# Linear attention beside a dense projection: the eighth group of scores behind the second unit of the tile in place of the first

## The chip, the cores and the metric

The kernel runs on one core of one Trainium2 chip. The metric is the device time of one execution in microseconds (us). Before the change it is 2720.19 us, the median of 3 runs (2718.54 to 2729.52).

## The reference, cut to what matters

Two transformer blocks over a sequence of 1024 tokens with width 1024, beside a context of 256 tokens. The first block is a gated linear attention in both directions with 4 heads (keys of 128, values of 256), together with a pooling branch; the second is a neighbourhood attention with a convolutional feed-forward part. The change touches the linear attention of the first block:

```python
p = h @ w_in                      # q, k, v, two low-rank gates, and the wide inputs zA, uB, zB, gA, gB
q, k = rope_2d(q), rope_2d(k)     # rotation by row and column
la = log_sigmoid(lowrank @ w_up + b) / 16        # decay per token and channel, forward and backward
...
diff = b[:, :, :, None, :] - b[:, :, None, :, :]  # b: cumulated decay
scores = einsum('bhid,bhjd,bhijd->bhij', q, k, exp(diff))   # within a chunk
S = exp(bC) * S + einsum('bhjd,bhjv->bhdv', k * exp(bC - b), v)   # state between chunks
```

## The kernel before

All work is written out engine by engine, each with its own queue in program order; semaphores join them. The dense products dominate. A weight tile (1024 x 128) is loaded by SP into `w_raw`, split by POOL into a high and a low part (`w_hi` L840, `w_lo` L843), and multiplied by TensorE as hi x hi + lo x hi + hi x lo. `pe_tile` (L484) does one tile: for each *unit* of 512 tokens `pe_unit` (L468, the matmuls at L478) issues 24 matmuls into one of two PSUM banks `pb`, and ScalarE evicts it (`store_tile`, L973). A unit waits for its bank (`bank_free`) and a tile for its split (`w_split`). The tile's first matmul raises `w_begun`, which lets POOL split the next tile. `pe_tile` takes a function `between`, which is called once, behind the first unit.

The first phase of the linear attention runs beside the dense tiles from number `T_ZA` on. It goes over ten chunks of 128 tokens: two of the context, without scores, and then eight of the sequence (`more`). Each chunk has three dense tiles of two units. In a chunk of the sequence, all 4 heads together:

- `p_gates` (L2691): the products for the decays (L2704) into banks 0 and 1 of `g`, and eight transposes of the values (L2712) into banks 2 and 3. The first wait for the fifth, the second for the seventh masked copy (`f_pred`) of the chunk before.
- VectorE then builds by levels, from small blocks to large, the keys and queries scaled by the decays (`f_first`, `f_grow`, L1880 to L1909), with ScalarE copying halves (`f_kept`); then two scans (`run`, L1959), two products for the state's keys (`kd`, L1964), and the masked copies.
- The scores within the chunk are made in eight *groups* (`p_scores`, L2715). Group 0 is the diagonal part, group m the level m - 1; each is one 128 x 128 product per head, into bank (m + 2) mod 6 of `g`. ScalarE copies group 0 into `pt` (L1152), and VectorE lays the groups 1 to 7 over it by seven masked copies (`f_choose`, L1932), each of which waits for its group (`f_lev`) and for the copy before it.
- Group 7 writes bank 3, which held group 1; so it waits for the first masked copy (L2736, `f_pred` at 7c + 1).
- `p_keys` (L2744): eight transposes of `kd` into banks 4 and 5 (L2753), which wait for `kd` and for the third masked copy.
- ScalarE stores `pt` behind the seventh copy, and then takes the transposed keys (`p_last`, L1096 to L1109).
- VectorE's queue goes on from the seventh copy to the rotation of the next chunk (`rope`, L1868 to L1871) and to the decays (L1945, L1880).

On TensorE, one chunk is: gates and value transposes, tile 0, tile 1, groups 0 to 3, first unit of tile 2, groups 4 to 7, second unit of tile 2, keys. After the last chunk TensorE goes on with the next dense tile; the other engines meet at the phase's end (`end_phase`), which ScalarE reaches when its stores have landed.

Of the kernel before, what the change touches and what calls it, by code (L numbers as in the profile page):

```python
# [95 lines left out]
def build(nc, modt, modw, cond, crow, cols, mats, tabs, hmask, inv, sgb, xT, ctxT, ctx2T, wall, wup, sgw, bias,  # L96
# [7 lines left out]
    with ctx:  # L104
# [296 lines left out]
        sq2, a = at("sq2", [P, 2, T], a)  # L401
        root2, a = at("root2", [P, T], a)
        _, a = at("xw", [P, KT, T], a)
        hh, a = at("hh", [P, 2, 2, T], a, F32R)
        hl, a = at("hl", [P, 2, 2, T], a, F32R)
# [56 lines left out]
        def step(base, i, by):  # L462

            return base if i is None else i * by + base
# [3 lines left out]
        def pe_unit(pe, b, xhi, xlo, tokens, kts, wcols, bank, ready=None):  # L468

            n = tokens.stop - tokens.start  # L470
            total, count = 3 * len(kts), 0
            first = None
            for k, wc in zip(kts, wcols):
                if ready is not None:
                    pe.wait_ge(xh_ready, ready + k)
                    pe.wait_ge(xl_ready, ready + k)
                for w, x in ((w_hi, xhi), (w_lo, xhi), (w_hi, xlo)):
                    mm = pe.matmul(pb[bank][:, 0:n], w[:, b, wc:wc + P], x[:, k, tokens],  # L478
                                   start=(count == 0), stop=(count == total - 1))
                    first = first or mm  # L480
                    count += 1
            return first, mm

        def pe_tile(pe, t0, i=None, tiles=0, units=0, xhi=None, xlo=None, ready=(), between=None, begin=0):  # L484

            b, u0 = t0 % 2, UNIT[t0]
            xhi, xlo = xhi or xh, xlo or xl
            pe.wait_ge(w_split, step(t0 + 1, i, tiles))
            for n in range(UNIT[t0 + 1] - u0):
                bank = (u0 + n) % 2  # L490
                pe.wait_ge(bank_free[bank], step((u0 + n) // 2 + 1, i, units // 2))
                tokens = slice(begin + n * H, min(begin + n * H + H, TA))
                first, last = pe_unit(pe, b, xhi, xlo, tokens, range(KT), range(0, 1024, P), bank,
                                      ready[n] if n < len(ready) else None)
                if n == 0:
                    first.then_inc(w_begun, 1)
                last.then_inc(unit_done, 1)
                if n == 0 and between is not None:
                    between()
# [129 lines left out]
        def rec(c, l, n):  # L629

            return REC * c + 2 + 5 * l + n
# [308 lines left out]
        def _(act):  # L940
# [561 lines left out]
            def at_heads(s):  # L1502

                i, (bc, br, _) = s // 16, step_of(s)
                act.wait_ge(at_ot, s // 2 + 1)
                if i >= 2 and s % 16 == 1:
                    act.wait_ge(kept_out, 96 + 16 * (i - 1))
                act.activation(at_tokens(br, bc)(heads_out[i % 2][:, :]),
                               g[:, 4, P:2 * P].rearrange("p (r c) -> p r c", c=16), ACT.Copy)\
                   .then_inc(at_ao, 1)  # L1510
                if s % 16 == 15 and i < 3:
                    act.wait_ge(at_ao, s // 2 + 1)
                    act.wait_ge(kept_out, 96 + 16 * i)
                    act.dma_start(ao_d[i], heads_out[i % 2][:, :]).then_inc(kept_out, 16)
# [1108 lines left out]
        def _(pe):  # L2623
# [67 lines left out]
            def p_gates(p):  # L2691

                b = p % 2
                if p == 0:
                    pe.wait_ge(tab_ready, 2)
                pe.wait_ge(p_in[b], 64 + (208 * (p // 2) if p >= 2 else 0))
                if p >= 1:
                    pe.wait_ge(p_la, p)
                if p >= 3:
                    pe.wait_ge(f_pred, 7 * (p - 3) + 5)  # L2700
                for d in range(2):
                    r = slice(32 * d, 32 * d + 17)
                    for h in range(HEADS):
                        mm = pe.matmul(g[:, d, CH * h:CH * h + CH], wup_sb[r, DK * h:DK * h + DK],  # L2704
                                       lrc[r, b, :], start=True, stop=True)
                mm.then_inc(p_gk, 1)
                if p >= 1:
                    pe.wait_ge(p_vt, p)
                if p >= 3:
                    pe.wait_ge(f_pred, 7 * (p - 3) + 7)  # L2710
                for n in range(8):
                    mm = pe.transpose(g[:, 2 + n // 4, CH * (n % 4):CH * (n % 4) + CH], vc[:, n, :], ident)  # L2712
                mm.then_inc(p_vtr, 1)

            def p_scores(p, groups):  # L2715

                c, b = CHUNKS[p], p % 2
                for m in groups:
                    l = m - 1
                    if m == 0:  # L2720
                        pe.wait_ge(p_kr, c + 1)
                        pe.wait_ge(p_qr, c + 1)
                        pe.wait_ge(p_vt, p + 1)
                    elif m == 1:
                        pe.wait_ge(f_rec, REC * c + 1)
                    else:
                        pe.wait_ge(f_rec, rec(c, l - 1, 2))
                        pe.wait_ge(f_cpy, CPY * c + 2 * l)
                    if m == 2:
                        pe.wait_ge(p_kt, p)  # L2730
                    if m == 4:
                        pe.wait_ge(p_la, p + 1)
                    if m == 6:
                        pe.wait_ge(f_diag, c + 1)
                    if m == 7:
                        pe.wait_ge(f_pred, 7 * c + 1)  # L2736
                    keys = kc[:, b] if m <= 1 else lk[:, l - 1]
                    queries = qc[:, b] if m == 0 else lq[:, l]
                    for h in range(HEADS):
                        mm = pe.matmul(g[:, (m + 2) % 6, CH * h:CH * h + CH], keys[:, h, :], queries[:, h, :],  # L2740
                                       start=True, stop=True)
                    mm.then_inc(f_lev, 1)

            def p_keys(p):  # L2744

                pe.wait_ge(p_kd, p + 1)
                if p >= 1:
                    pe.wait_ge(p_kt, p)
                if p >= 2:
                    pe.wait_ge(f_pred, 7 * (p - 2) + 3)  # L2750
                for d in range(2):
                    for h in range(HEADS):
                        mm = pe.transpose(g[:, 4 + d, CH * h:CH * h + CH], kd[:, d, h, :], ident)  # L2753
                mm.then_inc(p_ktr, 1)

            for p in range(NC):
                t0, more = T_ZA + 3 * p, CHUNKS[p] < NCX
                if p == 0:
                    pe_tile(pe, t0)
                p_gates(p)  # L2760
                if p:
                    pe_tile(pe, t0)
                pe_tile(pe, t0 + 1)
                if more:
                    p_scores(p, range(0, 4))
                    pe_tile(pe, t0 + 2, between=lambda: p_scores(p, range(4, 8)))
                else:
                    pe_tile(pe, t0 + 2)
                p_keys(p)
# [293 lines left out]
            for n in range(2):  # L3063
                for p in range(4):
                    t0 = T_W2 + 4 + 4 * n + p
# [57 lines left out]
            for n in range(2):  # L3123
                for m in range(KT):
                    t0, u = DOWN[last] + m // 4, DOWN_LAST + KT * n + m
# [150 lines left out]
```

## Time and profile before

| | |
|---|---|
| median of 3 runs | 2720.19 us |
| profiled execution, own time | 2720.14 us |
| its span | 2718.3 us |
| mean granted TensorE clock | 0.96 |
| TensorE busy | 2503.1 us, 92% |
| VectorE busy | 1498.0 us, 55% |
| GpSimd busy | 1058.7 us, 39% |
| ScalarE busy | 732.4 us, 27% |

The rows come from one profiled execution. Busy time says how long an engine worked, not whether anybody waited for it; the waits and the timelines say that. The eight chunks with scores lie between about 330 and 747 us of the span.

### The profile page before, as it was taken

The page shows a single profiled execution, that of the slowest core. Times are in us where ns is not written, and L with a number is a line of the kernel's source. Part 1 is how long each engine was busy: PE and PEld are TensorE (multiplying, and loading weights), DVE is VectorE, ACT ScalarE, POOL GpSimd, SP SyncE. Part 2 cuts the span into 40 slices and gives each one's busy share as a digit, 9 for nine tenths or more (in the row PEclk, how much of TensorE's full clock was granted, in tenths as well). Part 3 has the DMA queues.
Part 4 walks back from the last instruction along what each step waited for, and adds up shares of the span by engine and source line. Part 5 has one row for each costly group of instructions (what it writes and reads, how often), then busy time and mean ns, then how long its engine had stood idle before and what let it go on. Part 6 is the DMA issues. An engine that isn't in the chain of part 4 may idle for free.

```text
span 2718.3 us, 33036 instructions
## 1 busy us (share of the span) xinstructions
PE 2503.1 (92%) x12008; PEld 2048.8 (75%) x12008; DVE 1498.0 (55%) x2193; ACT 732.4 (27%) x1244; POOL 1058.7 (39%) x493
## 2 busy tenths in 40 slices
PE   8999999999889779999896899979889999999997
PEld 4888788788768757878675777868668888888885
DVE  4796155756611256554788644466764444444446
ACT  4411334344300045312322444432221111111112
POOL 2344333333347423447652011113554444444444
PEclk9999999999989889999997899979899999999998
DMA  9576444434266853233311231341211111111111
GB/s 350 190 258 224 157 144 140 139 124 152 91 243 216 303 189 143 86 130 123 131 47 53 70 100 58 96 159 44 69 60 47 47 47 48 52 46 46 46 46 70
DMA packets 131234, 325.25 MB, mean 120 GB/s; under 512 B 11569, under 2 KB 59249, under 8 KB 125617
## 3 DMA queue, kind: packets, MB, share of 16 engines
q1 hardware_dynamic: 91232, 215.63, 24.0%
q10 hardware_dynamic: 39888, 108.08, 11.1%
q8 instruction: 74, 1.21, 0.2%
q14 instruction: 40, 0.32, 0.0%
HBM read 248.57 MB, written 70.39 MB: 117 GB/s over the span
## 4 chain that ended last, share of the span: by engine, by line
PE 49%; DVE 8%; issue 3%; ACT 1%; DMA 1%; POOL 0%; DVEq 0%; SPq 0%; POOLq 0%; ACTq 0%
PE pb L478 35%; PE g L2978 6%; PE g L3051 2%; PE pb L2978 1%; DVE zcs L2249 1%; PE g L3031 1%; PE g L2959 1%; DVE f_spare L2458 1%; PE g L2838 1%; DMA kept_in<-cs_d 1%; DVE xl L2161 0%; PE g L2957 0%; DVE ml L2465 0%; DVE hl L2528 0%; DVE cb L2507 0%
## 5 line engine op out<-in xcount | busy, mean ns | idle before, releaser
L840 POOL TENSOR_TENSOR w_hi<-w_raw,one 128x1024 fp32r<-128x1024 f32 x191 | 401.1, 2100 | 1485.3 <-PE pb L478 1095.0
L843 POOL TENSOR_TENSOR w_lo<-w_raw,w_hi 128x1024 fp32r<-128x1024 f32 x191 | 515.2, 2697 | 14.9
L478 PE MATMUL pb<-xh,w_hi 128*128 128x512 f32 (+1 forms) x1224 | 481.4, 393 | 30.7 <-POOL w_lo L843 12.7
L478 PE MATMUL pb<-xh,w_lo 128*128 128x512 f32 (+1 forms) x1224 | 472.8, 386 | 0.0
L478 PE MATMUL pb<-xl,w_hi 128*128 128x512 f32 (+1 forms) x1224 | 472.1, 386 | 0.0
L478 PEld LDWEIGHTS pb<-xh,w_hi 128*128 128x128 f32 x1224 | 237.5, 194 | 79.9 <-POOL w_lo L843 13.9
L478 PE MATMUL pb<-mh,w_hi 128*128 128x512 f32 x704 | 279.0, 396 | 16.0 <-DVE ml L2465 7.3
L478 PE MATMUL pb<-mh,w_lo 128*128 128x512 f32 x704 | 276.2, 392 | 0.0
L478 PE MATMUL pb<-ml,w_hi 128*128 128x512 f32 x704 | 276.1, 392 | 0.0
L478 PEld LDWEIGHTS pb<-xl,w_hi 128*128 128x128 f32 x1224 | 235.9, 193 | 45.7
L478 PEld LDWEIGHTS pb<-xh,w_lo 128*128 128x128 f32 x1224 | 236.9, 194 | 43.8 <-issue 0.7
L478 PEld LDWEIGHTS pb<-mh,w_hi 128*128 128x128 f32 x704 | 133.5, 190 | 50.2 <-ACT mh L1605 11.7
L2551 DVE SCALAR_TENSOR_TENSOR x<-pb,modx,x 128x512 f32<-128x512 f32 x160 | 119.1, 749 | 89.2 <-PE pb L478 89.2
L478 PEld LDWEIGHTS pb<-ml,w_hi 128*128 128x128 f32 x704 | 133.6, 190 | 28.2
L478 PEld LDWEIGHTS pb<-mh,w_lo 128*128 128x128 f32 x704 | 133.9, 190 | 27.7 <-issue 0.5
L478 PE MATMUL pb<-hh,w_hi 128*128 128x512 f32 x352 | 138.8, 394 | 12.3 <-DVE x L2551 11.3
L2505 DVE TENSOR_SCALAR cb<-gp,col 128x1024 f32<-128x1024 f32 x22 | 43.6, 1984 | 189.8 <-ACT gp L1645 187.3
L973 ACT ACTIVATE stage<-pb 128x512 f32<-128x512 f32 x80 | 47.6, 597 | 335.0 <-PE pb L478 315.5
L478 PE MATMUL pb<-hh,w_lo 128*128 128x512 f32 x352 | 137.2, 390 | 0.0
L478 PE MATMUL pb<-hl,w_hi 128*128 128x512 f32 x352 | 137.0, 389 | 0.0
L1645 ACT ACTIVATE gp<-pb 128x512 f32<-128x512 f32 x40 | 24.0, 600 | 375.7 <-PE pb L478 375.7
L478 PE MATMUL pb<-bh,w_hi 128*128 128x512 f32 x256 | 102.8, 401 | 8.4 <-DVE bl L2108 4.7
(410 smaller groups left out, 4601.6 us busy)
## 6 DMA issues: line engine op xcount, KB each, us to landing
w_raw<-in_wall SPq DMA_DIRECT2D x190, 512.0 KB, 3.6
mod_later<-in_modw SPq DMA_DIRECT2D x28, 1024.0 KB, 6.4
proj_d<-stage ACTq DMA_DIRECT2D x40, 512.0 KB, 2.7
at_bias<-in_bias SPq DMA_DIRECT2D x64, 192.0 KB, 2.9
mod_raw<-in_modt SPq DMA_DIRECT2D x8, 1024.0 KB, 11.0
w_raw<-in_wall ACTq DMA_DIRECT2D x15, 512.0 KB, 6.6
svt<-vt_d ACTq DMA_DIRECT2D x12, 512.0 KB, 4.6
vc<-proj_d SPq DMA_DIRECT2D x10, 512.0 KB, 6.1
```

Source lines behind the costliest of these rows:

```text
L478: mm = pe.matmul(pb[bank][:, 0:n], w[:, b, wc:wc + P], x[:, k, tokens], start=(count == 0), stop=(count == total - 1))
L840: nc.gpsimd.tensor_tensor(w_hi[:, b, :], w_raw[:, b, :], one[:, 0:1].to_broadcast([P, 1024]), ALU.mult).then_inc(w_high, 1)
L843: nc.gpsimd.tensor_tensor(w_lo[:, b, :], w_raw[:, b, :], w_hi[:, b, :], ALU.subtract).then_inc(w_split, 1)
L973: act.activation(rows[:, b, lo:hi], pb[u % 2][:, 0:hi - lo], ACT.Copy, scale=scale)\
L2249: nc.vector.scalar_tensor_tensor(zcs[:, t, :], hpad[:, t, bass.ds(tap, T)], col[:, bass.ds(tap + (cw + TAPS * t), 1)], zcs[:, t, :], ALU.m ...
L2458: nc.vector.scalar_tensor_tensor(f_spare[:, 4 + k % 3, :], x2[:, k, half_of(n)], gain[:, 0, k:k + 1], f_spare[:, 2 + n, :], ALU.mult, ALU. ...
L2505: v = nc.vector.tensor_scalar(cb[:, kt, :], gp[:, kt, 0:T], w, None, ALU.mult)
L2551: nc.vector.scalar_tensor_tensor(x2[:, m, half], pb[u % 2][:, :], modx[:, 64 + m:65 + m], x2[:, m, half], ALU.mult, ALU.add).then_inc(bank ...
L2838: mm = pe.matmul(g[:, u, :], mean_v, osq[:, v, H * u:H * u + H], start=(v == 0), stop=(v == 1))
L2959: pe.matmul(g[:, s % 2, 0:HL], low, local(keys[rows, :]), start=False, stop=True)
L2978: mm = pe.matmul(dst[:, 0:n], w[:, t0 % 2, at_k:at_k + P], x[:, k, tokens], start=(begun and k == kts[0] and w is w_hi and x is xhi), stop ...
L3051: mm = pe.matmul(g[:, 4, 64 * j:64 * j + 64], ptr[:, s % 2, P * c:P * c + P], v, start=(c == 0), stop=(c == 4))
```

## The change

In a chunk of the sequence, groups 4 to 6 stay between the two units of tile 2, and group 7 is issued behind the second unit, in front of the keys' transposes. All else, the waits of each group among it, stays.

```diff
                 if more:
                     p_scores(p, range(0, 4))
-                    pe_tile(pe, t0 + 2, between=lambda: p_scores(p, range(4, 8)))
+                    pe_tile(pe, t0 + 2, between=lambda: p_scores(p, range(4, 7)))
+                    p_scores(p, range(7, 8))
                 else:
                     pe_tile(pe, t0 + 2)
                 p_keys(p)
```

## Rows read from the trace of the kernel before

**Rows 1.** The page's first part: busy us, share, instructions, by engine.
```profile
PE 2503.1 (92%) x12008; PEld 2048.8 (75%) x12008; DVE 1498.0 (55%) x2193; ACT 732.4 (27%) x1244; POOL 1058.7 (39%) x493
```

**Rows 2.** Waits of TensorE, 380 to 742 us: total, times, longest.
```profile
PE g L2740 <- DVE pt L1932: 27.0, 8, 3.4
```

**Rows 3.** Timeline of TensorE, one chunk: start, duration, instruction, idle time before it.
```profile
477.21 1.05 PE L2740 MATMUL g<-qc,kc 128*128 128x128 f32 x8
...
480.69 0.48 PE L478 MATMUL pb<-xh,w_hi 128*128 128x512 f32 x1
...
486.23 2.84 PE L2740 MATMUL g<-lq,lk 128*128 128x128 f32 x24
492.45 2.05 PE L2740 MATMUL g<-lq,lk 128*128 128x128 f32 x8 [3.38 <-DVE pt L1932]
...
500.36 1.03 PE L2753 MATMUL g<-mat,kd 128*128 128x128 f32 x8
...
502.96 1.09 PE L2712 MATMUL g<-mat,vc 128*128 128x128 f32 x8
503.81 0.48 PE L478 MATMUL pb<-xh,w_hi 128*128 128x512 f32 x1
```

**Rows 4.** Timeline of VectorE in the same chunk and the next.
```profile
486.01 4.46 DVE L1959 TENSOR_TENSOR_SCAN run<-av,reset 128x516 f32<-128x516 f32 x2
...
491.59 0.72 DVE L1932 COPY_PREDICATED pt<-mask,g 128x512 f32<-128x512 int32 x1
...
496.18 0.73 DVE L1932 COPY_PREDICATED pt<-mask,g 128x512 f32<-128x512 int32 x1
...
496.81 0.68 DVE L1868 TENSOR_TENSOR kc<-kc,tab 128x512 f32<-128x512 f32 x1
...
508.62 1.23 DVE L1945 SCALAR_TENSOR_TENSOR soft<-g,soft 128x1024 f32<-128x1024 f32 x1 [7.88 <-ACT soft L1123]
```

**Rows 5.** Windows: length, busy us by engine, granted clock (PEclk), DMA share, GB/s.
```profile
492.40:494.20 1.80, 1.75 (x9) 1.78 (x9) 1.72 (x6) 0.00 (x0) 0.00 (x0) 0.50 0.06 20
...
496.00:500.00 4.00, 4.00 (x19) 3.28 (x18) 3.92 (x8) 0.00 (x0) 0.00 (x0) 1.00 0.00 0
120.00:160.00 40.00, 40.00 (x229) 35.27 (x228) 37.95 (x46) 8.93 (x14) 17.58 (x6) 1.00 0.80 287
```

**Rows 6.** Windows from group 4 to the keys, eight chunks: first, last, sum.
```profile
387.78:403.27 15.49, 12.13 (x58) 10.40 (x56) 14.17 (x24) 1.00 (x2) 3.14 (x1) 0.78 0.19 69
...
731.28:745.53 14.25, 10.88 (x57) 9.43 (x56) 10.43 (x18) 1.01 (x2) 3.15 (x1) 0.88 0.21 74
sum 117.24, PE 90.24 PEld 78.06 DVE 108.37 ACT 8.10 POOL 25.19; mean PE 11.28 PEld 9.76 DVE 13.55 ACT 1.01 POOL 3.15
```

**Rows 7.** Timeline of ScalarE in the chunk of rows 3.
```profile
477.40 0.60 ACT L973 ACTIVATE stage<-pb 128x512 f32<-128x512 f32 x1 [1.00 <-PE pb L478]
...
502.17 1.02 ACT L1104 ACTIVATE spare_l<-g 128x1024 f32<-128x1024 f32 x1 [1.01 <-PE g L2753]
```

**Rows 8.** Timeline of ScalarE at the phase's end.
```profile
746.79 0.44 ACTq L1101 DMA_DIRECT2D pt_d<-pt  x1
747.34 1.03 ACT L1104 ACTIVATE spare_l<-g 128x1024 f32<-128x1024 f32 x1 [1.01 <-PE g L2753]
...
753.12 0.35 ACTq L1169 DMA_DIRECT2D skb<-kt_d  x1
```

**Rows 9.** Timeline of VectorE at the phase's end: the last masked copy.
```profile
741.23 0.73 DVE L1932 COPY_PREDICATED pt<-mask,g 128x512 f32<-128x512 int32 x1
```

**Rows 10.** Timeline of POOL: both halves of one split, the first of the next.
```profile
481.34 3.71 POOL L840 TENSOR_TENSOR w_hi<-w_raw,one 128x1024 fp32r<-128x1024 f32 x1 [10.17 <-PE pb L478]
485.13 4.25 POOL L843 TENSOR_TENSOR w_lo<-w_raw,w_hi 128x1024 fp32r<-128x1024 f32 x1
504.38 1.90 POOL L840 TENSOR_TENSOR w_hi<-w_raw,one 128x1024 fp32r<-128x1024 f32 x1 [15.00 <-PE pb L478]
```

**Rows 11.** Timeline of SP's queue: the last of the next chunk's loads.
```profile
525.97 0.43 SPq L698 DMA_DIRECT2D vc<-proj_d  x1
```

## The prediction

> **What bounds the kernel now.** I read the page's busy shares first: TensorE is busy 92% of the span, so time comes either out of its work or out of the 8% in which it stands [rows 1]. Then the waits of TensorE over the stretch of the change: there is a single line in them, the scores of L2740 waiting for the masked copy into `pt`, 27.0 us in 8 waits, the longest 3.4 us [rows 2]. So between 380 and 742 us TensorE is the pace of everything, except in one place per chunk. The timeline of one chunk shows the place: groups 4 to 6 start at 486.23 us, and group 7 at 492.45 after 3.38 us of idleness; the second unit of the dense tile, which needs nothing of this, stands behind group 7 in the same queue [rows 3]. What group 7 waits for is in VectorE's timeline: the first masked copy, at 491.59 us, which reads the bank that group 7 will overwrite. In front of it stand two scans that take 4.46 us together, and two products [rows 4].
>
> The stall costs more than its length. From 492.4 to 494.2 us the granted clock is 0.50 of full speed, so TensorE is at the lower of its two levels (1.2 of 2.4 GHz); from 496 us it is 1.00 again [rows 5]. Group 7 and the second unit together take 500.36 - 492.45 = 7.91 us [rows 3].
>
> **The change part by part.** Nothing is added or removed: in each of the 8 chunks that have scores, the 8 matmul records of group 7 (the page counts two for each of the four heads) trade places with the 24 matmuls of the second unit. No DMA and no semaphore of SP or POOL is in what moves; `unit_done` is raised earlier and `f_lev` for group 7 later against it.
>
> *TensorE.* At the full clock a group costs 0.87 us (four groups from 477.21 to 480.69 us are 3.48) and a unit 5.54 us (480.69 to 486.23) [rows 3]. From the start of group 4 to the keys' transposes (L2753) there will be four groups and one unit: 3.48 + 5.54 = 9.02 us, if nothing waits. That stretch took 15.49 us in the first chunk, 14.25 in the last, and 117.24 in all eight [rows 6]. Against 8 x 9.02 = 72.2 us that is 45.1 us less, of which 27.0 is the wait and 18.1 the lower clock behind it.
>
> *Does the second unit wait for something else?* It would start at 486.23 + 3 x 0.87 = 488.8 us. Its bank was emptied by the eviction that started at 477.40 us and took 0.60, nearly 11 us before [rows 7]. Its weights are the tile's, in use already. So no.
>
> *Does group 7, now behind the unit, wait or come late?* It would run from 494.4 to 495.3 us. The copy that it needs ends at 491.59 + 0.72 = 492.3. Its own reader, the seventh masked copy, starts at 496.18 us only because six others of 0.76 us stand in front of it [rows 4]. Slack 0.9 us: VectorE's chain keeps its times.
>
> *What is late next.* The chunk's tail moves up by 5.1 us, so its waits must be looked at anew. Keys at 495.3 need the third copy (over at 493.9). The gates (L2704), behind the eight records of the keys and so not before 496, need the fifth, over at 491.59 + 4 x 0.765 + 0.73 = 495.4. The value transposes (L2712) start 2.60 us behind the keys now (502.96 - 500.36), so at 497.9, and need the seventh, 496.18 + 0.73 = 496.9 [rows 3, 4]. Each finds it done, with 0.6 to 1.4 us to spare. This is the thin cover on which I cost the move at nothing; if the copies came d us later than this margin, the chunk would pay d, up to 8 d.
>
> *ScalarE.* Behind the unit's eviction it waits for the seventh copy to store `pt`, and only then takes the keys: 496.9 + 0.55 = 497.5 us in place of 502.17, so 4.7 us earlier where TensorE is 5.1 earlier [rows 7, 8]. The missing 0.4 us ends in the chain of `soft`; VectorE needed that at 508.62 us after 7.88 us of idleness [rows 4], and the next step, the exponential behind the next eviction, hangs on TensorE. Cost nothing for seven chunks. In the last chunk there is no next tile in front of the phase's end: ScalarE takes the keys at 747.34 us, and issues the next phase's first load at 753.12 [rows 8]. There the last copy starts at 741.23 us [rows 9], so the keys can be taken from 741.23 + 0.73 + 0.55 = 742.5 on: this chunk gives 4.8 us and not 14.25 - 9.02 = 5.2.
>
> *POOL and SP.* The split for the next tile (481.34 to 489.38 us) is used from 498.7 instead of 503.81: 9 us of slack remain. The next split starts behind that tile's first matmul, as now [rows 10]. The next chunk's loads are issued up to 525.97 us [rows 11], one chunk of 49 us earlier up to about 477, and first read by the rotation at 496.81 [rows 4]; both keep their distance from each other, some 19 us. No wait.
>
> *A rule weighed.* While the scans ran, POOL's halves of the split took 3.71 and 4.25 us; with VectorE idle the first half took 1.90 [rows 10]. After the change the last two or three rotation products (they start at 496.81 us [rows 4]) fall on the split that will start at about 499.3. The Trainium skill, "SBUF — State Buffer", section "Who interferes with whom", says that a VectorE instruction with two SBUF inputs and a GpSimd instruction that reads SBUF exclude each other, whoever issues second being blocked for the whole of the first. By that page each of these products could wait out a half of the split. By the rows, the worst for POOL is the 8 us that the pair takes beside the scans, in front of weights needed 11 us after the tile's start, and VectorE, done with the rotation at about 501, has 3 us until `soft` is due (508.62 less 4.7) and some 6 more until the next exponential. The sum is the same by both.
>
> **Sum.** Seven chunks: 117.24 - 14.25 - 7 x 9.02 = 39.8 us, and the last 4.8: 44.7 us. The profiled execution took 2720.14 us around a span of 2718.3, and the median of the runs is 2720.19, so both are the same base. 2720.1 - 44.7 = 2675.4 us. Later phases start together and should shift as a whole; where their stretches meet the clock's changes may move them by a few us either way. Bounds of the unmeasured: from 0 (the clock does not fall at all) to all of the 18.1 us (it stays low as now), and 0 to 2 us of a new wait per chunk. I take 0 for both: the clock is 1.00 where TensorE is busy 40 us in 40 (120 to 160 us) [rows 5], and the copies have their margin.
>
> **The rivals.**
> 1. *Only the idleness goes.* The clock falls in the same places although TensorE no longer stands. For it: the rows show the clock at 0.50 only after the stall, not why. Against: 1.00 over 40 us of full load. It gives 2720.1 - 27.0 = 2693 us.
> 2. *A new wait takes the place of the old one.* The seventh copy comes after TensorE reaches the value transposes. For it: 0.9 us of margin, and the copies stand behind scans whose length depends on POOL. Against: the distance from group 4 to the old wait's end is the same in all chunks (the longest wait 3.4, the mean 27.0 / 8 = 3.4 [rows 2]). At 1 to 2 us each it gives 2683 to 2691.
> 3. *The unit is held until where it starts now,* by some wait that no row shows. Then group 7 is last: the seventh copy ends at about 502.0 us, the keys' eviction goes from 502.17 to 502.5, and the chunk takes up to 0.9 us more: 2720 to 2727.
> 4. *Slower: the clock falls because TensorE no longer pauses.* Eight chunks last 8 x 43 = 347 us in the new form. A stretch at the lower level loses half its length, so 89 us of them at 1.2 GHz undo the gain and 116 us make it slower by over 0.5%. At 40% of the stretch it would be 139 / 2 = 69 us lost: 2745. Against it speaks the same row at 1.00.
>
> **How the numbers follow.** Full effect 80% (its own range 2670 to 2681), only the idleness 6%, a new wait 8%, held 3%, slower by the clock 3%. Range 2669 to 2689, which takes in most of rival 2 and leaves the others out. A difference under 0.5% (13.6 us) can't be told from no change here. Faster by more: 94%; within: 4%; slower: 2%.
>
> **What would show it.** Right: no idle time in front of L2740 in TensorE's waits; from group 4 to the keys 9.0 us; a granted clock near 1.00 over the eight chunks; a chunk every 43.4 us in the mean in place of (731.28 - 387.78) / 7 = 49.1 [rows 6]; VectorE's first copy still about 5.4 us behind the start of group 4. Wrong: a wait of L2712 or L2704 for the copies (rival 2), 0.5 clocks without a stall in front (rivals 1 and 4), or the second unit starting more than 3 us behind group 6 (rival 3).

## The result, and the profile after

The changed kernel took 2677.89 us in the median of four runs (2672.53 to 2682.41), against 2720.35 us before: a ratio of 0.9836, 95% interval 0.9817 to 0.9856. Measured twice more, on two chips, it was 2673.76 us against 2718.50 (ratio 0.9845, 0.9824 to 0.9865) and 2673.59 us against 2726.65 (0.9820, 0.9797 to 0.9842). So it is 1.6 to 1.8% faster, some 45 us; 2675.4 was forecast. Its times come in two groups: of 14, ten lie at 2671.6 to 2674.6 us, three at 2682.1 to 2685.0, and one between. The kernel before scatters in the same way: of 39 times, 27 lie at 2715.3 to 2722.9 us and 12 at 2725.0 to 2730.7. The profiled execution below is of the upper group: 2682.14 us, span 2680.4.

The waits of TensorE over the eight chunks (375 to 697 us), where [rows 2] had 27.0 us in 8 waits, are now an empty list. The timeline of the third chunk answers to [rows 3]: start, duration, instruction, and no idle time in front of any.

```profile
472.05 2.84 PE L2740 MATMUL g<-lq,lk 128*128 128x128 f32 x24
474.64 0.48 PE L478 MATMUL pb<-xh,w_hi 128*128 128x512 f32 x1
...
480.22 1.05 PE L2740 MATMUL g<-lq,lk 128*128 128x128 f32 x8
481.11 1.04 PE L2753 MATMUL g<-mat,kd 128*128 128x128 f32 x8
...
483.71 1.09 PE L2712 MATMUL g<-mat,vc 128*128 128x128 f32 x8
484.56 0.47 PE L478 MATMUL pb<-xh,w_hi 128*128 128x512 f32 x1
```

The windows from group 4 to the keys (length, busy us by engine, granted clock, DMA) answer to [rows 6]: first, last and sum of the eight.

```profile
385.20:394.27 9.07, 9.07 (x58) 8.08 (x57) 8.90 (x14) 1.61 (x3) 3.15 (x1) 1.00 0.35 118
...
689.14:698.21 9.07, 9.07 (x58) 8.08 (x57) 8.90 (x14) 1.61 (x3) 3.15 (x1) 1.00 0.32 116
sum 72.53, PE 72.53 PEld 64.59 DVE 71.16 ACT 12.88 POOL 25.24; mean PE 9.07 PEld 8.07 DVE 8.89 ACT 1.61 POOL 3.16
```

The reader is to see that TensorE is busy 9.07 us of 9.07 at a clock of 1.00 in every chunk. 117.24 - 72.53 = 44.7 us went here.

VectorE in the same chunk answers to [rows 4]. Its copies stand where they stood: the first 5.35 us behind the start of group 4 (before: 491.59 - 486.23 = 5.36).

```profile
477.40 0.73 DVE L1932 COPY_PREDICATED pt<-mask,g 128x512 f32<-128x512 int32 x1
...
482.05 0.72 DVE L1932 COPY_PREDICATED pt<-mask,g 128x512 f32<-128x512 int32 x1
...
482.68 0.67 DVE L1868 TENSOR_TENSOR kc<-kc,tab 128x512 f32<-128x512 f32 x1
...
485.19 2.38 DVE L1869 TENSOR_TENSOR qs<-qs,tab 128x512 f32<-128x512 f32 x1
487.61 2.78 DVE L1871 TENSOR_TENSOR qc<-qc,qs 128x512 f32<-128x512 f32 x1
490.31 1.21 DVE L1945 SCALAR_TENSOR_TENSOR soft<-g,soft 128x1024 f32<-128x1024 f32 x1
```

ScalarE at the phase's end answers to [rows 8]. It takes the keys at 700.34 us in place of 747.34, now released by the seventh copy and not by the keys, and issues the next phase's first load at 704.98 in place of 753.12.

```profile
699.91 0.33 ACTq L1101 DMA_DIRECT2D pt_d<-pt  x1
700.34 1.03 ACT L1104 ACTIVATE spare_l<-g 128x1024 f32<-128x1024 f32 x1 [2.23 <-DVE pt L1932]
...
704.98 0.35 ACTq L1169 DMA_DIRECT2D skb<-kt_d  x1
```

From there the profiled execution is 48.1 us ahead, more than the eight chunks gave: its first scores already start 2.6 us earlier (376.18 us against 378.75), which the change doesn't reach, and the next phase's first load is issued 3.39 us behind the store of the keys (701.59) where it was 4.53 (748.59). At its end it is 37.9 us ahead. Of the 10.2 us that are lost between, 8.5 are lost behind the first step of the second block's attention (which starts at 1466.74 us, and at 1513.14 in the kernel before), by TensorE's clock. The experiments look into that last.

### The profile page after: what moved, and what is told of

Same layout as the page of the kernel before. It is cut to its first block, busy times and chain, and to the rows that moved or that the text cites. A ratio compares the mean times of both kernels' runs of the same rounds, so it can differ in the third digit from the quotient of the medians.

```text
span 2680.4 us, 33036 instructions
## 1 busy us (share of the span) xinstructions
PE 2496.2 (93%) x12008; PEld 2044.2 (76%) x12008; DVE 1518.1 (57%) x2193; ACT 731.1 (27%) x1244; POOL 1062.3 (40%) x493
## 4 chain that ended last, share of the span: by engine, by line
PE 50%; DVE 8%; issue 3%; ACT 1%; DMA 1%; POOL 0%; DVEq 0%; SPq 0%; POOLq 0%; ACTq 0%
PE pb L478 36%; PE g L2979 6%; PE g L3052 2%; PE pb L2979 1%; DVE zcs L2249 1%; PE g L3032 1%; PE g L2960 1%; DVE f_spare L2458 1%; PE g L2839 1%; DMA kept_in<-cs_d 1%; PE g L2958 0%; DVE ml L2465 0%; DVE xl L2161 0%; DVE hl L2528 0%; DVE cb L2507 0%
```

## Experiments

**The changed kernel again,** for a profile of the lower group.

> The changed kernel once more, unaltered. Its four times fell into two groups, 2672.5 to 2673.6 and 2682.1 to 2682.4 us. Theory: the phase of the scores is the same in all of them (9.07 us from group 4 to the keys in each chunk, no wait before L2740), and the 9.5 us between the groups lie at the start of the second block's attention, where the profile taken so far shows TensorE's clock at 0.50 for 41 us in one piece, in place of 10.2 and 3.4 us in the kernel before. Expected: times in one of these groups or both; a profile of about 2672 us, if one comes, differs from the first mainly between the attention's first step and its fourth. Rival: the 9.5 us come from the phase of the scores or its end (stalls in some chunks); then the stretch from group 4 to the keys differs between the profiles.

Five times: 2671.59 to 2674.63, and one of 2684.98. The profile fell on a run of 2673.24 us. Windows of it, over the attention's start:

```profile
1462.50:1472.50 10.00, 7.36 (x30) 6.24 (x29) 6.19 (x18) 5.36 (x14) 0.00 (x0) 0.50 0.34 111
1472.50:1482.00 9.50, 5.97 (x46) 5.11 (x45) 6.91 (x14) 3.21 (x8) 0.00 (x0) 0.99 0.08 21
1482.00:1487.00 5.00, 4.92 (x26) 4.39 (x26) 4.25 (x10) 1.44 (x5) 2.88 (x2) 0.66 0.23 49
1487.00:1511.00 24.00, 22.43 (x142) 18.91 (x142) 14.60 (x41) 11.24 (x27) 1.38 (x1) 1.00 0.28 81
```

and of the first profile, over the same work:

```profile
1463.00:1465.00 2.00, 0.70 (x4) 0.29 (x2) 1.89 (x8) 0.77 (x1) 0.00 (x0) 0.89 0.25 63
1465.00:1505.00 40.00, 37.15 (x148) 32.67 (x149) 24.75 (x51) 13.65 (x39) 4.25 (x2) 0.50 0.26 75
1505.00:1515.00 10.00, 10.00 (x62) 8.45 (x61) 4.35 (x15) 3.34 (x8) 0.00 (x0) 0.97 0.06 20
```

The two profiles' first steps of the attention start within 0.7 us of each other (1466.10 and 1466.74 us), and the ends of their spans lie 9 us apart (2671.4 and 2680.4). In both TensorE has no wait in the eight chunks. So the groups are two outcomes of the clock there, 0.50 for 10 us in one and for 40 us in the other, and the phase of the scores has no part in them. TensorE's last product and first step around the attention's first wait, in this profile and in the first, show where the two part:

```profile
1462.56 0.69 PE L2960 MATMUL g<-kb,ql 64*128 64x384 f32 x1
...
1466.10 1.33 PE L3032 MATMUL g<-mat,pr 128*128 128x128 f32 x5 [2.64 <-ACT pr L1499]
```

```profile
1463.14 0.45 PE L2960 MATMUL g<-kb,ql 64*128 64x384 f32 x1
...
1466.74 1.33 PE L3032 MATMUL g<-mat,pr 128*128 128x128 f32 x5 [3.04 <-ACT pr L1499]
```

Where the low clock lasts 10 us it has begun in front of the wait: the product takes 0.69 us in place of 0.45, and the wait is 2.64 us. Where it lasts 40 us the product still ran at the full clock, and the wait is 3.04 us. Ten of the profiles have no added products at this wait, and all ten fall on one side or the other. From the first step to the end they take 1205.2 to 1205.3 us in four (the kernel before, the changed kernel in two profiles, and the next experiment) and 1213.6 to 1213.7 in six (the first profile, the early copy, group 7 behind the keys, and the three with late copies, all below). So the upper group costs 8.4 us behind that step, whatever the kernel. Why the clock falls sooner in one execution than in another no run shows.

Since the profile of before had 0.86 over the 50 us from 1507.5, as this one has from 1461, the honest comparison of profiles is 2718.3 with 2671.4: 46.9 us.

**The wait filled and not removed.** The kernel before, with:

```diff
                     if m == 7:
+                        fill = UNIT[T_ZA + 3 * p + 2] + 1
+                        pe.wait_ge(bank_free[fill % 2], fill // 2 + 1)
+                        for _ in range(4):
+                            for h in range(HEADS):
+                                pe.matmul(pb[fill % 2][:, CH * h:CH * h + CH], kc[:, b, h, :], qc[:, b, h, :],
+                                          start=True, stop=True)
                         pe.wait_ge(f_pred, 7 * c + 1)
```

> The kernel before, with 16 needless products (four groups' worth, 32 records, 3.48 us at the full clock) into the free bank of the dense tile while group 7 waits for the first masked copy. TensorE's wait is then filled and not removed. Theory (27 us idleness, 18 us lower clock behind it): the clock stays at 1.00, from group 4 to the keys 3.48 + 3.48 + 5.54 + 0.07 = 12.6 us per chunk, 8 x 12.6 = 101 us in place of 117.2, so about 16.5 us faster than before: 2703 us. Rival (the clock falls for another reason than the pause, or the 18 us are not clock): the stretch stays at 14 to 15.5 us and the time at 2720.

2701.39 us (2698.18 to 2702.81), ratio 0.9937 (0.9923 to 0.9951). The timeline shows the needless products at L2740 in the place of the pause:

```profile
481.35 2.84 PE L2746 MATMUL g<-lq,lk 128*128 128x128 f32 x24
484.02 3.74 PE L2740 MATMUL pb<-qc,kc 128*128 128x128 f32 x32
487.59 1.06 PE L2746 MATMUL g<-lq,lk 128*128 128x128 f32 x8
488.41 0.48 PE L478 MATMUL pb<-xh,w_hi 128*128 128x512 f32 x1
...
493.99 1.03 PE L2759 MATMUL g<-mat,kd 128*128 128x128 f32 x8
```

The window over it, from group 4 to the keys, has a clock of 1.00:

```profile
481.35:493.99 12.64, 12.64 (x90) 11.60 (x89) 12.35 (x22) 1.01 (x2) 3.13 (x1) 1.00 0.25 85
```

12.64 us, where the eight of before lay between 14.06 and 15.49, with group 7 no earlier than before. The kernel before had a median of 2718.5 us beside it, so 17 us are the clock alone. The pause causes the lower clock, and the forecast's split into 27 us of standing and 18 of clock holds.

**The first copy in front of the scans.** The kernel before, TensorE untouched:

```diff
                     f_last(c, p)
+                    f_choose(c, 0)
...
                 if more:
-                    for l in range(LEVELS):
+                    for l in range(1, LEVELS):
                         f_choose(c, l)
```

> The kernel before with TensorE's order untouched; VectorE makes the first masked copy in front of the two scans and not behind the two products. Theory (group 7 waits for nothing but this copy, and the copy stands behind the scans only by its place in the queue): the copy is over about 1.4 us behind the start of group 4, group 7 at 2.6 us doesn't wait, the clock stays at 1.00, and the stretch from group 4 to the keys is 9.0 us as in the changed kernel: about 2675 us, equal to it within its own scatter of 9 us. Rival (the second unit in front of group 7 is what brings the gain, since something else also holds group 7): a wait before L2740 of 1 us or more remains and the time stays above 2690.

2674.56 us (2671.84 to 2684.89), ratio 0.9834 (0.9821 to 0.9847): the same gain without moving group 7. In TensorE's timeline all 32 records of groups 4 to 7 run in one piece:

```profile
474.63 3.73 PE L2741 MATMUL g<-lq,lk 128*128 128x128 f32 x32
...
483.70 1.03 PE L2754 MATMUL g<-mat,kd 128*128 128x128 f32 x8
```

Group 7 was held by that one copy, and the copy by its place behind the scans.

**The margin of the copies.** The changed kernel, with the products for `kd` made needlessly often in front of the copies (six more here, four in the second form; `p_more` is a new semaphore):

```diff
+                dve.wait_ge(p_run, 2 * p + 2)
+                if p:
+                    dve.wait_ge(p_ktr, p)
+                for n in range(6):
+                    dve.wait_ge(p_more, 6 * p + n)
+                    nc.vector.tensor_tensor(kd[:, n % 2], kc[:, b], run[:, n % 2, :, 1 - n % 2:1 - n % 2 + CH],
+                                            ALU.mult).then_inc(p_more, 1)
+                dve.wait_ge(p_more, 6 * p + 6)
```

> The changed kernel, with the two products for kd made four times in place of once, in front of the masked copies (each of the six more waits for the one before): the copies come 6 x 0.65 = 3.9 us later, a little more with the waits. Theory (the move costs nothing only because the copies have a margin of 0.9 us): what goes beyond the margin is paid in each chunk. 3.9 - 0.9 = 3.0 us in seven chunks and 3.9 in the last, 25 us, if the clock stays at 1.00: 2703 us; more where the new waits of TensorE (before group 7, the keys or the gates) lower the clock, up to the 18 us that this cost before. Rival (the margin is much wider than the timelines say, the copies being covered by what follows them on TensorE): under 8 us slower.

2708.43 us in the median (2706.49 to 2709.19 in five runs, 2743.83 in the sixth, which is the profiled one). Waits of TensorE in it, from 375 to 750 us (total, times, longest):

```profile
PE g L2749 <- DVE pt L1933: 16.8, 7, 2.4
PE g L2762 <- DVE pt L1933: 2.8, 7, 0.4
```

The first copy starts at 500.20 us, 9.84 us behind group 4 in place of 5.35: 4.5 us later. The first wait is of group 7 for the first copy: its margin of 494.4 - 492.3 = 2.1 us, as forecast for group 7 itself, leaves 2.4. The second is of the keys. In all eight chunks TensorE waits 22.4 us (2.8 each), which is less than the 25 us expected although each product took 0.72 us and not 0.65: behind the wait the clock is low, the keys' records take 1.87 us where they took 0.96 in the changed kernel, and the gates, which would have waited for the fifth copy, come late enough by themselves. The common time lies 34.7 us over 2673.7, so the waits don't explain it alone.

> The delay experiment with four needless products for kd in place of six. In the profile of the longer one each cost 0.72 us with its wait, the copies came 4.5 us later, and TensorE waited 2.8 us per chunk (2.4 before group 7, 0.4 before the keys). Theory: the copies come 3.0 us later here; group 7 has 2.1 us to the first copy, so it waits 0.9 us, and the keys 0.4 us for the third: 1.3 us per chunk, 3 us in the last, about 12 us over the changed kernel's 2673.7: 2686 us, without a lower clock. Rival (any pause of TensorE in this place lowers its clock as the old one did): 1.3 + 2 us per chunk and over 2700 us.

2703.87 us, in two groups (2692.4 and 2692.5; 2701.3 to 2707.9); 2686 was expected, a miss. Waits of TensorE in its profile, from 375 to 730 us:

```profile
PE g L2749 <- DVE pt L1933: 5.6, 6, 1.0
PE g L2713 <- DVE pt L1933: 3.4, 7, 0.5
PE g L2762 <- DVE pt L1933: 3.2, 8, 0.4
PE g L2749 <- ACT pt L1153: 1.7, 2, 0.8
...
```

The gates (L2713), which I had left out of this expectation, wait 0.5 us too; together the rows make 13.9 us. The lower group lies 18.8 us over 2673.7, so 5 us are not found in the waits; no profile fell on it. Four of the six times are over 2700, as the rival had it, but for another reason in part, which the windows below show.

> The longer delay once more, for a second profile: five of its six times were 2706.5 to 2709.2 us, while its profile fell on the one of 2743.8, with the clock at 0.50 for 10.2 us in each of seven chunks. Theory: in the common case the waits are the same (2.8 us per chunk, 22 us) and the clock falls in few of the chunks or for shorter; 2708 - 2673.7 - 22 - 1 = 11 us of lower clock are left to find. Rival: the waits themselves are longer.

This time 2708.27 to 2733.97 us, median 2718.37 in eight runs on another chip, as slow as the kernel before (ratio 1.0000, 0.9980 to 1.0021). Whether the six times before it were a narrow sample or the chip plays a part isn't shown: on both chips the kernel before has the same median (2718.5 and 2718.35). The profile fell on one of 2717.83. The wait before group 7 has the same length in both profiles, 2.4 us, but what follows it differs. A window of this profile behind the wait:

```profile
494.36:500.00 5.64, 5.64 (x38) 5.01 (x38) 5.48 (x12) 1.62 (x4) 0.50 (x1) 0.79 0.12 46
```

and one of the earlier profile:

```profile
502.61:512.90 10.29, 10.29 (x42) 8.98 (x43) 7.01 (x14) 6.19 (x8) 2.84 (x2) 0.52 0.22 76
```

The waits themselves are not longer (20.7 us in the eight chunks against 22.4); the rival stated for this run is out. Where the time goes is read from one window per profile, from the keys in front of the eight chunks to the keys of the last: the changed kernel (the lower group's profile), the kernel before, and the late copies in the order four, six again, six.

```profile
352.43:699.79 347.36, 347.36 (x1921) 299.52 (x1920) 260.79 (x455) 156.47 (x273) 136.79 (x48) 1.00 0.46 147
```

```profile
353.42:745.53 392.11, 365.11 (x1921) 312.85 (x1920) 242.21 (x458) 156.72 (x272) 132.88 (x48) 0.95 0.41 130
```

```profile
353.61:722.25 368.64, 354.73 (x1921) 301.85 (x1920) 285.09 (x485) 156.68 (x273) 132.04 (x48) 0.99 0.44 140
```

```profile
352.42:734.09 381.67, 360.98 (x1922) 308.01 (x1921) 298.44 (x501) 156.50 (x273) 131.66 (x48) 0.97 0.42 135
```

```profile
353.38:758.73 405.35, 382.95 (x1922) 326.41 (x1920) 273.48 (x500) 157.20 (x273) 132.90 (x48) 0.91 0.40 127
```

TensorE's work is the same in all five. Length less busy time is its idleness, and busy time beyond 347.36 us is the lower clock:

| profile | idle, us | lower clock, us |
|---|---|---|
| changed kernel | 0 | 0 |
| kernel before | 27.0 | 17.8 |
| four more products | 13.9 | 7.4 |
| six more, again | 20.7 | 13.6 |
| six more | 22.4 | 35.6 |

All three profiles with late copies also have the long piece of low clock at the attention, 8.4 us that come in kernels without late copies too. That is the rest of the miss: in the profile of 2706.77 us the eight chunks give 21.3 us over the changed kernel and the attention 8.4. So the theory of "no lower clock" is wrong, and the rival's 2 us of clock per chunk came in two of eight chunks only (two last 47.3 us, the others 45.2 to 45.8). Pauses of one length, 2.4 us in front of group 7, cost 13.6 us of clock in one profile and 35.6 in another. What decides it stays open.

**Group 7 still later.** The changed kernel, with the keys in front of group 7:

```diff
                     pe_tile(pe, t0 + 2, between=lambda: p_scores(p, range(4, 7)))
+                    p_keys(p)
                     p_scores(p, range(7, 8))
                 else:
                     pe_tile(pe, t0 + 2)
-                p_keys(p)
+                    p_keys(p)
```

> The changed kernel with group 7 one step later still, behind the keys' transposes. Theory (group 7 is free to come as late as the seventh masked copy wants it, 10.0 us behind the start of group 4): it would end at about 10.0 us, so the seventh copy comes 0 to 0.3 us later and ends at 10.7 to 11.0 us, still in front of the value transposes at 11.6: the same time as the changed kernel within 2 us, in each of its two groups. Rival (the margin of 0.9 us is not there): a wait before the value transposes (L2712) and 5 us or more slower.

TensorE has no wait in the eight chunks and they follow each other every 43.43 us (43.42 in the changed kernel). VectorE shows what was computed, the seventh copy now waiting for group 7 by 0.27 us:

```profile
482.50 0.72 DVE L1932 COPY_PREDICATED pt<-mask,g 128x512 f32<-128x512 int32 x1 [0.27 <-PE g L2740]
```

The margin is there. The median is 2683.09 us (2678.39 to 2684.86), and ratio 0.9859 (0.9837 to 0.9881): three of four times are those of the upper group, and one lies between the groups, so "within 2 us in each of its two groups" held for three. The profile, of 2682.47 us, has the long piece of low clock at the attention (granted clock 0.59 over the 50 us from 1461, as in the first profile from 1461.7), so the 9 us are not the price of the later group.

**The two groups.** The changed kernel, and needless products where TensorE stands 2.6 to 3.0 us in front of the attention's first step:

```diff
+            for _ in range(12):
+                pe.matmul(g[:, 2, 0:P], ident, mean_d, start=True, stop=True)
             for s in range(STEPS):
```

> The changed kernel, and 12 needless products of 128x128 (about 2.6 us at the full clock) in front of the attention's first step in the second block, where TensorE stands 2.6 to 3.0 us for the first exponential. Theory: the kernel's two groups of times (2672 and 2683) are two outcomes of the clock behind this pause, 0.50 for 10.2 and 3.4 us or for 41 us in one piece; with the pause filled the long piece does not come, all times lie in 2668 to 2675 us, and the median stays or falls by some us. Rival (the long piece has another source, such as the many small products of the attention): both groups remain, 9 to 10 us apart.

2673.18 us (2671.83 to 2676.45), none in the upper group. Since 10 of 14 times without the products would have done the same, that tells little alone. Its profile (2672.77 us) shows that the products don't keep the clock from falling here:

```profile
1455.00:1461.80 6.80, 5.46 (x19) 2.69 (x18) 4.16 (x6) 3.12 (x3) 0.00 (x0) 1.00 0.40 157
1461.80:1465.20 3.40, 3.40 (x15) 2.85 (x15) 2.28 (x10) 2.06 (x4) 0.00 (x0) 0.52 0.47 149
...
1479.00:1485.40 6.40, 4.63 (x19) 3.97 (x19) 5.06 (x11) 1.44 (x5) 2.02 (x2) 0.50 0.07 15
```

The clock falls at 1461.8 us, in front of the needless products (they start at 1462.90) and behind gaps of 0.79 and 0.56 us. With TensorE busy it is back after 3.4 us in place of 10. The products shorten the low clock; the theory of one pause that makes it is not borne out.

> Group 7 behind the keys, as in the experiment before, together with the 12 needless products in front of the attention's first step. With group 7 behind the keys alone, three of four times lay at 2682.5 to 2684.9 us. Theory (these are the slow group, made by the pause of TensorE in front of the attention's first exponential): at least four of five times fall to 2671 to 2677 us. Rival (group 7 behind the keys is itself 9 us slower, or the needless products don't touch the clock's choice): the times stay at 2678 to 2685 us.

2673.67 us (2671.58 to 2676.71): none in the upper group, where three of four had been. But this was another chip, on which the unaltered kernel had none in the upper group either (below), so the step from one to the other isn't shown to be the products'. The profile is like the last one: a clock of 0.52 over 1462.8 to 1466.2 us.

> The changed kernel with the 12 needless products once more: five times so far, 2671.8 to 2676.5. Theory: no time over 2678 in five more. Rival (the five were chance; of 14 times without the products, 4 were over 2682): one or two of five over 2680 us.

2677.93 us, from 2671.18 to 2681.52: four of five over 2677 and two over 2678, against the theory. The profile (span 2675.6) shows why. Here the clock stays at 1.00 for the first 17 us, and then is low for 24 us, all the same:

```profile
1463.00:1480.00 17.00, 14.46 (x104) 12.16 (x103) 11.12 (x31) 8.90 (x23) 0.00 (x0) 1.00 0.27 84
1480.00:1504.00 24.00, 21.32 (x79) 18.37 (x80) 15.88 (x30) 5.73 (x17) 4.24 (x2) 0.50 0.28 74
```

Around the boundary of the two windows stands the next pause, 3.04 us long:

```profile
1482.68 0.48 PE L2968 MATMUL g<-mat,osb 128*128 128x128 f32 x1 [3.04 <-DVE osb L2419]
```

> The changed kernel unaltered, as the measure for the other two on this chip. Theory: one or two of five times over 2680 us, the others 2671 to 2675. Rival: none over 2680, and then the products' effect can't be seen on this chip.

2672.86 to 2674.47 us in four, and 2679.59 in the fifth: the rival's case, so this chip could not show the products' effect. What stands: with the first pause filled, none of 15 times reached 2682 us, and without it 7 of 23 (the changed kernel, the first copy in front of the scans, and group 7 behind the keys) did. On one and the same chip that is only none of five against three of four, and of two different kernels. The piece of 40 us is in none of the three profiles with the pause filled; shorter pieces, at the first place or at the second, are in all three. What makes the two groups is open. A version that is faster than the changed kernel has not come out of it (2673.2 and 2677.9 against 2673.8 and 2673.6).

## Why the prediction was right, point by point

- *The number.* 2675.4 was forecast and 2677.89 measured, but no time lies there: the median stands between two groups, so its nearness is partly luck. The profile that the sum started from has the short piece of low clock at the attention, and its like among the new times are those of 2672.5 to 2673.6, about 2 us faster than forecast.
- *The place and the release.* Right: the single wait of [rows 2] is gone, nothing took its place. That it was one copy's place in VectorE's queue is shown by the early copy, which gains the same from the other side.
- *From group 4 to the keys 9.02 us.* Measured 9.07, eight times 72.53 against 72.2. A chunk comes every 43.42 us, forecast 43.4. The 45.1 us of the stretch came out as 44.7.
- *27 us of standing and 18 us of clock.* Shown by the filled wait: 17 us came back although TensorE did 32 needless records per chunk. Over the eight chunks the windows give 27.0 and 17.8.
- *The second unit does not wait, group 7 is not late, VectorE keeps its times.* All three right: the unit starts 2.59 us behind group 4, group 7 at 8.17, the first copy at 5.35.
- *The thin cover.* The margins held. They are real and small: copies 3.0 us later produced waits at group 7, the keys and the gates, 13.9 us in all. What the forecast had not priced is that such waits bring back some of the low clock, 7.4 us there.
- *ScalarE.* The keys' eviction runs 2.13 us behind the keys' start (483.24 - 481.11) where it was 1.81; the 0.3 us are hidden in the chain of `soft`, and the last chunk pays them. The next phase still gained 1.1 us more, as its first load is issued 3.39 us behind the keys' store and before 4.53. That was in no term of the sum. It goes with the new order and not with the execution: 3.4 to 3.8 us in all ten profiles with group 7 moved, 4.4 to 4.6 in the three without. Why is not shown.
- *The rule weighed.* Two products of the rotation took 2.38 and 2.78 us in place of 0.69 each, while POOL's split ran beside them: 3.8 us of blocking. The split in that chunk:

```profile
485.12 1.91 POOL L840 TENSOR_TENSOR w_hi<-w_raw,one 128x1024 fp32r<-128x1024 f32 x1 [9.92 <-PE pb L478]
487.11 2.73 POOL L843 TENSOR_TENSOR w_lo<-w_raw,w_hi 128x1024 fp32r<-128x1024 f32 x1
```

  Each product ends about 0.5 us behind a half of the split. The trace agrees with what the Trainium skill says in "SBUF — State Buffer", section "Who interferes with whom". It cost TensorE nothing, as both ways of the sum had it, but it used up the cover: VectorE had stood 7.88 us before `soft` and now goes on to it at 490.31 us without a pause. So it does in four of seven chunks; its waits for `soft` are 4.5 us in the other three together, and were 59.2 in seven.
- *Later phases shift as a whole, a few us either way.* This was the largest error: 10.2 us in the profiled execution, 8.5 of them from the clock at the attention's start, the size of the spread in the times. Nothing shows the change to cause it: the kernel before has times of an upper group too (12 of 39), though none of those was profiled. The own range of the likeliest case, 2670 to 2681, just misses the upper group of 2682 to 2685; the stated range of 2669 to 2689 holds it.
- *Rivals.* Only the idleness (2693): out, the clock is 1.00 in all eight windows. A new wait (2683 to 2691): out by the empty list of waits. Held unit: out by the start at 2.59 us. Clock falling without pauses: out in this phase (1.00 over all 347.36 us of the eight chunks).

## What to carry to other kernels

A wait in an in-order queue costs what stands behind it. If that needs nothing of the wait, let it go first, but count how late the delayed work may come: here its reader stood behind six copies and left 0.9 us. The same wait can be taken away from the other side, by moving the one instruction that releases it to the front of its queue. On TensorE, add to a pause the clock behind it, and read both from one window that begins and ends at a fixed instruction: length less busy time is the pause, and busy time beyond that of an undisturbed run is the clock. Here the clock was two thirds of the pause, but between half and 1.6 times of it in the profiles with late copies. Before two kernels are compared by one profile each, see whether a later stage far from the change took the same course in both.

## What the runs showed that I had not expected

- With TensorE busy 37 of 40 us (transposes, small products and products of 256 to 512 columns mixed), the clock stayed at 0.50 for the whole 40 us, and in another run of the same kernel, over the same instructions, it was back after 10 us. Which of the two comes is worth 8.4 us behind the first step. In all ten profiles with that wait unfilled it goes by whether the clock fell in front of that wait (then 2.6 us long) or not (then 3.0).
- A pause of 2.4 us per chunk was followed by a clock of 0.52 over 10 us in one run and 0.79 over 6 us in another; the times of that kernel went from 2706.5 to 2743.8 us. The changed kernel's 14 times span 13 us. A long pause need not scatter more: the kernel before, with 3.4 us per chunk, spans 15 us in 39 times.
